# Conditioning units of a two-layer transformer block: eight to a PSUM bank, forty of them after the gate tiles of layer 0

## The reference

```python
mod_l = silu(c) @ ada_w[l] + ada_b[l]          # 6 parts of 1024: sh1, sc1, g1, sh2, sc2, g2
mod_c = silu(c_ctx) @ ada_w[l] + ada_b[l]
u = rmsnorm(h, norm_g[l, 0]) * (1 + sc1) + sh1
p = u @ w_in[l]                                 # four branches: delta net, retention, attention, Fourier
acc = sum_i sigmoid(u @ w_gate[l, i] + b_gate[l, i]) * (y_i @ w_branch[l, i])
h = h + g1 * rmsnorm(acc @ w_out[l], norm_g[l, 1])
v = rmsnorm(h, norm_g[l, 2]) * (1 + sc2) + sh2
h = h + g2 * rmsnorm(ffn(v), norm_g[l, 3])      # layer 0: dense; layer 1: top-2 of 8 experts
```

## Time and profile before

| | |
|---|---|
| three runs | 2344.87, 2340.34, 2344.16 us |
| median | 2344.16 us |
| profiled execution, span from first to last instruction | 2341.8 us |
| profiled execution's own time beside its span | not recorded |
| TensorE busy | 2221.8 us, 95% |
| VectorE busy | 1438.4 us, 61% |
| ScalarE busy | 1160.3 us, 50% |
| bytes moved | 448.31 MB, 191 GB/s over the span |
| matmuls' share of the chain that ended last | 89% |

### The profile page before, as it was taken

One profiled execution on the slowest core, in us unless ns is written; L12 is line 12 of the kernel. 1 busy time (PEld: TensorE's weight loads), 2 busy tenths in 40 slices (PEclk: granted clock), 3 DMA queues, 4 the chain that ended last, 5 costly groups with the idle time before them and its releaser, 6 DMA issues.

```text
span 2341.8 us, 37971 instructions
## 1 busy us (share of the span) xinstructions
PE 2221.8 (95%) x15802; PEld 1833.5 (78%) x15802; DVE 1438.4 (61%) x2102; ACT 1160.3 (50%) x1616; POOL 121.4 (5%) x94
## 2 busy tenths in 40 slices
PE   6998989999998999998988899889999999999998
PEld 4767868778787888886766799778888888888886
DVE  2125667444333222335566566378999999899998
ACT  3224443323223222325254354267878778787787
POOL 0000332000000000000014200000000000000000
PEclk9999999999999999999989999979999999999999
DMA  8874002322204222221200164259989899998995
GB/s 335 324 319 169 1 2 94 127 98 100 90 2 165 91 90 103 95 90 56 91 1 1 56 236 162 108 221 350 359 330 374 342 346 359 340 368 338 348 361 213
DMA packets 63326, 448.31 MB, mean 191 GB/s; under 512 B 7216, under 2 KB 8240, under 8 KB 9520
## 3 DMA queue, kind: packets, MB, share of 16 engines
q1 hardware_dynamic: 60880, 434.86, 48.7%
q10 hardware_dynamic: 2272, 10.97, 1.2%
HBM read 443.71 MB, written 2.10 MB: 190 GB/s over the span
## 4 chain that ended last, share of the span: by engine, by line
PE 89%; DVE 4%; ACT 3%; issue 2%; DMA 1%; POOL 1%; PEld 0%; DVEq 0%; SPq 0%; ACTq 0%; PEldq 0%; POOLq 0%
PE bank L1176 11%; PE bank L1277 10%; PE bank L657 9%; PE bank L638 7%; PE bank L640 7%; PE bank L639 7%; PE bank L1285 5%; PE bank L811 4%; PE bank L756 4%; PE bank L1213 4%; PE bank L492 3%; PE bank L768 2%; PE bank L682 2%; PE bank L1196 2%; PE bank L577 1%
## 5 line engine op out<-in xcount | busy, mean ns | idle before, releaser
L2130 DVE TENSOR_TENSOR wsp_l<-ring,wsp_h 128x1024 fp32r<-128x1024 f32 x528 | 639.5, 1222 | 40.5 <-ACT wsp_h L1388 9.2
L1388 ACT CAST wsp_h<-ring 128x1024 fp32r<-128x1024 f32 x528 | 555.2, 1054 | 151.7 <-PE bank L640 89.8
L638 PE MATMUL bank<-wsp_h,xTs_h 128*128 128x512 f32 x704 | 283.8, 403 | 2.5 <-DVE xTs_l L2122 2.5
L640 PE MATMUL bank<-wsp_h,xTs_l 128*128 128x512 f32 x704 | 276.4, 393 | 0.0
L639 PE MATMUL bank<-wsp_l,xTs_h 128*128 128x512 f32 x704 | 275.2, 391 | 0.0
L2678 DVE TENSOR_TENSOR dsp_l<-ring,dsp_h 128x1024 fp32r<-128x1024 f32 x66 | 80.8, 1225 | 240.1 <-ACT dsp_h L1824 240.1
L1824 ACT CAST dsp_h<-ring 128x1024 fp32r<-128x1024 f32 x66 | 69.1, 1048 | 256.1 <-PE bank L1277 181.6
L1176 PE MATMUL bank<-u_hi,gsp_h 128*128 128x512 f32 (+1 forms) x512 | 174.3, 340 | 1.2 <-DVE arena L2602 1.2
L1176 PE MATMUL bank<-x_lo,gsp_h 128*128 128x512 f32 (+1 forms) x512 | 171.7, 335 | 0.0
L1176 PE MATMUL bank<-u_hi,gsp_l 128*128 128x512 f32 (+1 forms) x512 | 171.5, 335 | 0.0
L2236 DVE TENSOR_TENSOR ring_lo<-ring,win_hi 128x1024 fp32r<-128x1024 f32 x44 | 56.1, 1277 | 167.9 <-ACT win_hi L1524 165.2
(11 more groups left out here) (371 smaller groups left out, 4327.4 us busy)
## 6 DMA issues: line engine op xcount, KB each, us to landing
ring<-in_moe_tiles_dram SPq DMA_DIRECT2D x264, 1024.0 KB, 4.9
ring<-in_ada_tiles_dram SPq DMA_DIRECT2D x48, 1024.0 KB, 11.1
ring<-in_ffn_tiles_dram SPq DMA_DIRECT2D x33, 1024.0 KB, 4.8
ring<-in_gate_tiles_dram SPq DMA_DIRECT2D x32, 1024.0 KB, 6.2
ring<-in_in_tiles_dram SPq DMA_DIRECT2D x22, 1024.0 KB, 4.9
arena<-in_branch_tiles_dram ACTq DMA_DIRECT2D x8, 1024.0 KB, 8.2
ring<-in_out_tiles_dram SPq DMA_DIRECT2D x8, 1024.0 KB, 4.8
halfc<-in_halfc_dram SPq DMA_DIRECT2D x1, 1040.0 KB, 18.4
```

The source lines that it names most:

```text
L638: pe.matmul(o, xTs[0][:, kk, :], whi[:, k, :], start=(kk == 0), stop=False)
L640: mm = pe.matmul(o, xTs[1][:, kk, :], whi[:, k, :], start=False, stop=(kk == KD - 1))
L1388: act.copy(wsp[0][:, g % 4, :], half_slot(MOE0, g)).then_inc(s.gq_o.up, 1)
L2130: v.tensor_tensor(wsp[1][:, g % 4, :], half_slot(MOE0, g), wsp[0][:, g % 4, :], ALU.subtract).then_inc(s.gq_pt.up, 1)
```

## The change

1. **Accumulation.** `silu_c` gets 46 columns per chunk, zero but for two. A product takes the 32 columns from `2 * (GROUP - 1 - j)` on, so that unit j of a group lands in rows 2j and 2j + 1 of the same bank. Eight units (`GROUP`), or two in the opening, accumulate in one bank, and one copy and one pair of column matmuls serve all of them.
2. **Place.** The 40 later units stand no more behind the windows; four stand behind each of the gate slots 4 to 13 of layer 0 (`ADA_GATES`). Their rows go to bank 2 and their columns to bank 3; so in layer 0 the branch products always go to banks 6 and 7, and wait for `mg_add(2 * g)`. Conditioning tiles are freed by a semaphore of their own (`ada_free`). ScalarE copies a group's rows at q = 15, 19, 23, 27 and 31, and VectorE modulates two rounds later.
3. **Opening.** The eight early units go in four pairs (256 columns of part 0 and the same of part 1). Chunks 0 to 5 are transposed first, pairs 2 and 3 and chunks 6 and 7 come between the two halves of window 0. VectorE and ScalarE work chunk pair by chunk pair. The input's two halves are loaded first on two queues, and small constants come in one load (`early`); other constants come behind later windows.

```diff
+        PAIRS = PER_PART
+        EARLY = [u + PER_PART * part for u in range(PAIRS) for part in range(2)]
+        LATE = [u for u in range(DEPTH * NADA) if u not in EARLY]
+        GROUPS = len(LATE) // GROUP
...
+            for g in range(MW // 2):
+                GATE_SLOT[l].append(len(slots))
+                slots.append((d["gate_tiles"][l, 3 - g // 4, g % 4], (KD, CW)))
+                if l == 0 and g in ADA_GATES:
+                    ada_slots(LATE[4 * (g - ADA_GATES[0]):4 * (g - ADA_GATES[0] + 1)])
...
+        def free_at(n):
+
+            if n in ADA_SLOT:
+                return ada_free, ADA_SLOT.index(n) + 1
+            return slot_free, n + 1 - sum(a < n for a in ADA_SLOT)
...
-                    sp.wait_ge(slot_free, n - RING + 1)
+                    sp.wait_ge(*free_at(n - RING))
...
+            def ada_products(n, rows_at, j, size):
...
+                    r = 32 * (k % 4)
+                    mm = pe.matmul(bank[rows_at][r:r + 32, 0:CW], silu_c[:, k, at:at + 32], w[:, k, :],
+                                   start=(j == 0 and k < 4), stop=(j == size - 1 and k >= 4))
+                mm.then_inc(ada_free, 1)
...
+                            late = l == i == 0 and half == 1
+                            if late:
+                                ada_pair(2)
+                                ada_columns(2, 7, 2)
+                                ada_pair(3)
+                                prenorm_T(s, (6, 7))
+                                ada_columns(3, 7, 2)
...
-                        if i and ada_after(l, i - 1):
-                            ada_columns(ada_after(l, i - 1)[-1])
...
+                def ada_between(g):
+
+                    done = 4 * (g - ADA_GATES[0])
+                    if done > 0 and done % GROUP == 0:
+                        ada_columns(PAIRS + done // GROUP - 1, 3, GROUP)
+                    if g in ADA_GATES:
+                        for u in range(done, done + 4):
+                            i = PAIRS + u // GROUP
+                            if u % GROUP == 0:
+                                pe.wait_ge(ada_row, i)
+                            ada_products(len(EARLY) + u, 2, u % GROUP, GROUP)
+
...
-                                mm = transpose(bank[6 + c][:, P * t:P * (t + 1)], un[:, t, P * c:P * (c + 1)])
+                                mm = transpose(bank[(2 if ctx_out else 6) + c][:, P * t:P * (t + 1)], un[:, t, P * c:P * (c + 1)])
...
+                        if ctx_out:
+                            pe.wait_ge(*(s.mg_add(2 * g) if g else s.st_oa(8)))
...
+                            at, o, ob = slice(P * c, P * (c + 1)), (3 - br) % 2, bank[(6 if ctx_out else b + 2) + m][:, lo:TOK]
...
+                        if l == 0:
+                            ada_between(g)
...
+                pe.wait_ge(mod_ok, PAIRS + GROUPS)
...
-                    for k in range(1, KD, 2):
-                        evacuate(l, 0, s.tp1, s.u_odd, range(NT), k)
-                        if k == 1:
-                            weight_high(0)
-                        input_high(k - 1)
+                    for j in range(PAIRS):
+                        if j >= 2:
+                            ada_copy(j, 6, 2 * j + 2)
+                        act.wait_ge(mod_ok, j + 1)
+                        evacuate(l, s.tp1, s.u_odd, 2 * j + 1)
+                        input_high(2 * j)
+                        input_high(2 * j + 1)
+                        if j < 2:
+                            weight_high(j)
...
+                    if l == 0 and q in ADA_DONE:
+                        i = ADA_DONE.index(q)
+                        ada_copy(PAIRS + i, 2, len(EARLY) + GROUP * (i + 1))
...
-                    for k in range(0, KD, 2):
-                        evacuate(l, 0, s.tp1, s.u_even, range(NT), k)
-                        if k == 0:
+                    for j in range(PAIRS):
+                        if j:
+                            modulate_pair(j)
+                        v.wait_ge(mod_ok, j + 1)
+                        evacuate(l, s.tp1, s.u_even, 2 * j)
+                        input_low(2 * j)
+                        input_low(2 * j + 1)
+                        if j == 0:
                             weight_low(0)
...
+                    if l == 0 and q - 2 in ADA_DONE:
+                        modulate_group(ADA_DONE.index(q - 2))
```

More of the change, by code:

```diff
@@ L41 @@
 NADA = 6 * D // CW
-FIRST = 2 * D // CW
-ADA = DEPTH * NADA
+PER_PART = D // CW
+GROUP = 8
+ADA_GATES = range(4, 14)
 RING = 6
@@ L307, in build_program, with ada_slots @@
                [OFF_RET + 256 * i for i in range(4)])
[L309 to L320, removed]
+        PAIRS = PER_PART
+        EARLY = [u + PER_PART * part for u in range(PAIRS) for part in range(2)]
+        LATE = [u for u in range(DEPTH * NADA) if u not in EARLY]
+        GROUPS = len(LATE) // GROUP
+        slots, ADA_SLOT, GATE_SLOT, GATES, OUT, WIN_SLOT = [], [], [], [], [], []
+        def ada_slots(units):
+            for u in units:
+                ADA_SLOT.append(len(slots))
+                slots.append((d["ada_tiles"][u // NADA, u % NADA], (KD, CW)))
         for l in range(DEPTH):
@@ L405, in build_program, with chunk_bank @@
         SCAN = (tuple(range(2 * NT)), (3, 2, 1, 0, 7, 6, 5, 4))
+        ADA_DONE = [2 * (ADA_GATES[0] + 2 * i + 1) + 5 for i in range(GROUPS)]
+        def chunk_bank(k):
+            return k if k < 6 else k - 2
         def half_slot(n, q):
@@ L492, in transpose, with prenorm_T @@
                 return pe.transpose(dst, src, ident)
[L494 to L502, removed]
+            def prenorm_T(s, some):
+                for k in some:
+                    if k >= 6:
+                        pe.wait_ge(*(s.u_odd if k % 2 else s.u_even)(k // 2))
+                    for t in range(NT):
+                        last = transpose(bank[chunk_bank(k)][:, P * t:P * (t + 1)], xs[:, t, P * k:P * (k + 1)])
+                    last.then_inc(s.tp1.up, 1)
             def next_T(s, below, g):
@@ L749, in _ @@
                             if c0 < OFF_Z or c0 == OFF_F:
[L750 to L760, removed]
+                                for ks in ((4, 5), (6, 7)) if late else (range(4 * half, 4 * half + 4),):
+                                    for m in range(2):
+                                        for k in ks:
+                                            if i == 0 and m == 0:
+                                                pe.wait_ge(*s.x_lo(k + 1))
+                                            a = CW * (k % 4) + P * m
+                                            for p, (x, u) in enumerate(((0, u_hi), (0, x_lo), (1, u_hi))):
+                                                mm = pe.matmul(bank[(unit + m) % 4][:, P * toks[0]:TOK], w[x][:, a:a + P],
+                                                               u[:, k, P * toks[0]:TOK],
+                                                               start=(k == 0 and p == 0), stop=(k == KD - 1 and p == 2))
+                                        if k == KD - 1:
+                                            mm.then_inc(s.win_mm.up, 1)
                             else:
@@ L2034, in modulation, with modulate_pair, modulate_group @@
                 return v.tensor_tensor(dst, raw, gain, ALU.mult)
+            def modulate_pair(j):
+                v.wait_ge(ada_sum, j + 1)
+                for part in range(2):
+                    ins = modulation(0, part, bank[7][:, 4 * part:4 * (part + 1)], 2 * j, 2)
+                ins.then_inc(mod_ok, 1)
+            def modulate_group(i):
+                v.wait_ge(ada_sum, PAIRS + i + 1)
+                for e in range(2):
+                    l, part = (LATE[GROUP * i + PER_PART * e]) // NADA, LATE[GROUP * i + PER_PART * e] % NADA // PER_PART
+                    ins = modulation(l, part, bank[3][:, 16 * e:16 * (e + 1)])
+                link(ins)
+                v.sem_inc(mod_ok, 1)
             def gate_diag(l, sub, g_d, streams):
@@ L2627, in _ @@
                     merge(n)
+                    if l == 0 and n == MW - 3:
+                        modulate_group(GROUPS - 1)
                 v.wait_ge(*s.gb_m1(2 * len(streams)))
```

241 lines of the change are left out of this document (109 added, 132 removed).

## The result

| | before | after |
|---|---|---|
| median | 2342.61 us (4 runs, 2340.34 to 2344.87) | 2396.08 us (4 runs, 2394.34 to 2397.93) |
| ratio, 95% interval | | 1.0229 [1.0214, 1.0244] |
| span of the profiled execution | 2341.8 us | 2392.6 us |
| mean granted clock | 0.976 | 0.962 |

The changed kernel is 53.5 us slower by the medians and 50.8 by the spans. The forecast was 2399 us.

A forecast was written before the change was run, and what follows sets the result against it. TensorE's work and waits were taken to bound the kernel: -63.2 - 2.5 - 0.5 + 41.3 + 48.6 + 12.8 + 18 = +54.5 us, on the span of 2341.8 plus 2.4, gives 2399 us; range 2352 to 2424.

The forecast's parts named there:

- Bound: Whole kernel: TensorE, busy 95% of the span, sets the time by what it does or waits for.
- Windows: Layer 0, window 0's end to the Fourier step: without units, windows follow each other in 11.73 us; gain 63.2 us.
- The rival that they don't speed up: Layer 0 windows: splits, convolution and constants bind them, 3 us each over eight; +24, 2423 us; chance 5%.
- Opening: Start to window 0's end: input loaded first, but VectorE serves chunk pairs strictly in order; gain 2.5 us.
- Modulations: VectorE's middle stage: ten later modulations move to its idle time beside the gates; gain 0.5 us.
- Products and columns: Layer 0 gate stage: 40 products at 0.965 and five column pairs at 0.54 us; loss 41.3 us.
- The queue: Gate slots 5 to 13: branches wait behind late gate tiles, 9 x 5.4 = 48.6 us, plus 12.8 for two branch splits.
- The clock: Behind the gate-stage waits: the granted clock falls after TensorE idles, 2.0 us in each of nine slots, 18 us.
- The burst: Gate stage tile loads: the fourth tile of a burst lands 14.1 us after the burst's first issue.
- the lower bound of 12.1: Gate stage bursts: fourth tile lands at 12.1 us, wait 3.4, no lost clock; as a rival 2363 us, chance 14%.
- the gates keep pace: Gate stage: tile g+1 lands by R + 9.8 (R: previous slot's branches end), nothing waits; -24.9, 2319 us; chance 13%.

The follow-up runs named there:

- gate_tile_first: Changed kernel with gate tile g+1 listed ahead of the four unit tiles of slot g instead of behind them; 2318.55 us, ratio 0.9896 to the kernel before.
- gate_tile_third: Changed kernel with gate tile g+1 listed ahead of the last of slot g's four unit tiles, third of its burst; 2355.14 us, ratio 1.0055.
- second_low_early: Changed kernel with the low part of window 0's second weight half made behind the first two pairs' inputs instead of all four; 2390.35 us, ratio 1.0207.
- sigmoids_copies_first: Changed kernel, list untouched, layer 0's sigmoids, merges and group-row copies moved ahead of the late gate tile's cast or low part; 2318.03 us, ratio 0.9896.
- sigmoids_first: Changed kernel, list untouched, layer 0's sigmoids ahead of the late gate tile's cast and merges ahead of its low part; 2330.81 us, ratio 0.995.

## Why the prediction was right

- **Bound.** That TensorE's path sets the time at both ends held: the difference is made of what was added to that path, what was taken from it, and its waits.
- **Windows, -63.2.** Measured -62.7, with the forecast distance of 11.73 us between windows and L837's successor at 141.63 (forecast 139 to 143). The rival that they don't speed up fell.
- **Opening, -2.5.** Measured -0.9. The second half did start at 49.97 for the forecast 49.7 and behind `ring_lo`. What I missed is that this wait costs a second time, in the clock: I had window 0 end 6.8 us after that start, and it took 8.09, at 0.50 up to 54.9.
- **Modulations, -0.5.** Measured +0.5 for the whole middle stretch: within what the same stretch varies by between the traces (210.9 to 217.6), so the runs say nothing on so small a term.
- **Products and columns, 41.3.** Measured 39.8 in `gate_tile_first`: products 0.90 each in a row of four instead of 0.965, column pairs 0.35 instead of 0.54, 37.7 together; the other 2 are gate matmuls at up to 11.20 behind the products instead of 10.97.
- **The queue, 48.6 + 12.8 = 61.4.** Measured 56.8 in nine waits: seven of 4.8 to 5.1 us for the 5.4, and the two with the split 11.3 and 10.9 for 11.8. The mechanism is shown from both sides, by the list and by the engines' order. The cast began at R + 14.6 instead of R + 15.2, since the burst took 13.5 us for the 14.1 (below); the branch started at R + 19.6 for R + 20.3. Distances between branches are 24.3 to 25.6 us and 31.7 and 31.3 in two, as forecast, but for the first, 22.4, whose branch ahead (slot 4's) still ran at the full clock.
- **The clock, 18.** Measured 20.0: 2.2 a slot for the 2.0. The Trainium skill ("TensorE: Matmul & The Clock Gate", Why this matters for your kernels) has TensorE fall back to half rate between bursts; the branches at 4.33 to 5.49 us after 4.8 to 5.1 us of idle agree, twice 2.77 being 5.54, and the granted clock of 0.50 at 444.20 to 450.80. Idles of 1.1 to 1.6 us in `gate_tile_third` left the clock at 1.00, one of 1.9 didn't.
- **The burst.** The gate tile landed 13.5 us after the burst's first issue (426.8 to 440.3), for the 14.1 that I took and the lower bound of 12.1. That these agree so well is in part luck: the bursts before lost 4.2 us between their first and second tile (landings at 63.9 and 68.1), where these take 2.5, and the new ones have their long step at the fourth. The Trainium skill ("DMA: Bandwidth & Descriptors", Anatomy of one DMA), by which the estimate was 11.6, isn't borne out for four tiles; its section is on transfers that GpSimd issues, and these are SyncE's. For three it is nearer: by the page an estimate of 9.2 us, measured 9.7 (426.8 to 436.5).
- **Not foreseen.** 5.0 us were gained in the rest. In layer 1, between the first window and the gate stage, where no instruction of TensorE was changed, it was 6.7 (250.0 us before and 243.3 after), and some of it was lost again elsewhere. The windows, before, then after:

```profile
1107.90:1357.90 250.00, 217.16 (x3235) 0.95 0.13 48
```
```profile
1164.60:1407.90 243.30, 212.44 (x3235) 0.96 0.13 49
```

The number of matmul records is the same, and TensorE needed 4.7 us less for them. In windows of some 40 us, length times (1 - clock) adds up to 13.5 us before and 9.0 after, so the granted clock accounts for 4.5 us of the 6.7. `gate_tile_first`, `second_low_early` and `sigmoids_copies_first` have 250.4, 247.3 and 245.3 us there, so nothing shows it to be a gain of the change. What decides it in an execution stays open.

By the spans the forecast was 2341.8 + 54.5 = 2396.3, and 2392.6 came, 3.7 less: 3.4 from the gate stage and 5.0 from the rest, against 1.6 in the opening, 0.5 in the windows, 1.0 in the middle stretch and 1.7 behind the gates (where TensorE was busy 68.0 us for 66.3, at a granted clock of 0.94 for 1.00). That the sum came as near as its largest terms is in part chance, above all the 5.0. The median lay 3.5 above the profiled span where I had put 2.4; both set a median beside the span of one run, and the time of a run lies 1.8 above its own span (2394.39 and 2392.6 in the profiled one). The rival *the gates keep pace* is what the cured kernels do: its 2319 us, worked out as windows and opening against products, was met by `gate_tile_first` (2318.55) and `sigmoids_copies_first` (2318.03). Its condition was named in the prediction (the gate tile first), but the changed kernel doesn't meet it.

## What to carry to other kernels

When work is spread into a busy stage with its data in one strictly ordered list, look for which tile now lands late against its first use, and then at everything that stands behind the instruction that waits for it, on each engine: a tile that is only needed a slot later can hold up this slot. It is enough to break the chain at one place: put the tile that others queue behind first, or put the work that is ready ahead of the instruction that waits. An idle TensorE of some 5 us is to be priced at 7, since what follows runs at the lower clock; one of 1.9 to 2.5 us cost 1.7 to 2.8 us more in the matmuls behind it, and one of 1.0 to 1.6 us hardly more than itself. And a difference of a few microseconds far from the edit is to be set beside the spread of the same kernel's runs before it is explained.

## What the runs showed of the hardware

- 1 MB tiles that SyncE issued 0.9 us apart landed 2.4 to 2.5 us apart (changed kernel, slots 5 to 13; one step was 2.8), but for one step of 3.5 to 3.9 us in each burst, which came with a 16 KB packet on the instruction queue: ahead of the fourth tile in the changed kernel (a gate tile) and in the burst shown of `gate_tile_third` (a conditioning tile), ahead of the third in the burst at 429.7 of `sigmoids_first`.
- After TensorE idled 4.65 us, 24 matmuls took 8.09 us instead of about 5.65, and after 4.8 to 5.1 us twelve took 4.33 to 5.49 instead of 2.77, with the granted clock at 0.50. After 7.2 to 11.4 us they took 5.13 to 5.44, no more. After 1.1 to 1.6 us they took 3.00 to 3.07 at a clock of 1.00, and after 1.9 us 4.58.
- The same instructions took 243 to 250 us in layer 1 of these traces, and 210.9 to 217.6 in the middle stretch of layer 0. For the two traces compared there the granted clock accounts for about the whole difference. Runs of one kernel differ by as much (2337.88 to 2346.09 us in nine), so a single trace does not tell a kernel's part in it.
